# Products without a reader inside a blockwise inversion, and a reordered beginning of the first head group

## The chip, the cores and the metric

The kernel runs on one NeuronCore of a Trainium2 chip. The metric is device time in microseconds of one execution; the time before is 2007.33 us, the median of 3 runs from 2003.42 to 2015.3 us. TensorE (PE) multiplies, VectorE (DVE), ScalarE (ACT) and GpSimd (POOL) work elementwise, SyncE (SP) issues most transfers. Each engine runs its own instructions in order and waits on semaphores for the others.

## The reference, cut to what matters

512 tokens of width 1024 pass a first block (pooling, stick-breaking attention, a squared-ReLU MLP), then 16 meta tokens are put in front (T = 528) and a gated delta layer and a latent attention layer follow. The change touches the gated delta layer (16 value heads on 8 key heads, chunks of the sequence):

```python
def gdn_mixer(h, w_in, conv_w, a_log, dt_bias, out_norm, w_out):
    proj = h @ w_in
    qkv, z, b, a = ...                       # 4096, 2048, 16 and 16 columns
    qkv = jax.nn.silu(causal_depthwise_conv(qkv, conv_w))      # 4 taps
    q = l2norm(...) * (GDN_DK ** -0.5); k = l2norm(...); v = ...
    beta = jax.nn.sigmoid(b)
    g = -jnp.exp(a_log) * jax.nn.softplus(a + dt_bias)
    o = gated_delta_rule_chunked(q, k, v, beta, g)
    ...
def gated_delta_rule_chunked(q, k, v, beta, g):
    gc = jnp.cumsum(g, axis=-1)
    decay = jnp.exp(jnp.where(incl, gc[..., :, None] - gc[..., None, :], -jnp.inf))
    m = jnp.einsum('bhnid,bhnjd->bhnij', kb, k) * jnp.where(strict, decay, 0.0)
    sol = lax.linalg.triangular_solve(m + eye, rhs, left_side=True, lower=True, unit_diagonal=True)
    ...                                      # then a scan over the chunks
```

## The kernel before

Activations lie feature-major: 128 features on the partitions, 8 slices (kt) of a width of 1024, tokens along the columns. Products of weights and activations are kept near fp32 by splitting both into a high and a low part: `mm3` (L325 to L329) multiplies high by high, high by low and low by high. A weight panel of 128 output features is 512 KB; SP loads it (`refill`, L592), ACT writes its high half (`split_high`, L317), POOL its low half (`split_low`, L322), in a ring of four, and PE counts up `panel_used` when it is through. A projection of a panel over all 528 tokens is `project(j, b, k0, k1)`: 8 slices, each 2 halves of the tokens x 3 products = 6 products of 264 columns, 48 in all, into two PSUM banks.

The gated delta layer works in four groups of four value heads (`gdn_group`, g = 0 to 3, unrolled on every engine). The tokens form 5 chunks: 1 to 4 of 128 tokens, chunk 0 the 16 meta tokens. In each group:

- Panels 0 to 7 are projected (two of k, two of q, four of v). For each, DVE applies the four taps of the convolution (`taps`, L1477 and L1484), ACT and DVE the SiLU (`conv_exp`, `conv_clamp`, `lnexp`, `gated`), and for k and q a norm over the head (`l2_square`, `l2_sum`, `l2_rsqrt`, `l2_scale`).
- The decays: the running sums of the gates, one row per head and chunk, are split into high and low, written to a buffer in memory (`g_home`) and read back as rows (`decays_in`, L615). PE spreads them over a bank (`decay_rows`, L2169), ACT makes exp(-|difference|) of them (`decays`, L1002 and L1006).
- `first_m` (L1521) makes the matrices M of chunks 1 to 4 from the grams of k, the decays and beta. M goes through memory (`m_home`) to a layout with one 16x16 block per partition, in which POOL inverts the diagonal blocks by elimination (L693, L697); the inverses come back by way of `w_home`.
- The inversion: 15 steps, s = 0 to 14 (`STEPS`: levels 4, 5, 6, and in each the chunks 1, 2, 3, 4, 0), join blocks of 16 to 32, 64 and 128. A step is a product q (L2355, L2350 or L2359) with a mask times M from POOL (L721, L728), an ACT copy of it, one step later a second product (`join`: L2303, L2298, L2307), a DVE subtraction, and two steps later for levels 4 and 5 a transpose (`turn_u`, L2324) with a DVE copy (L1644). Level 4 is done in halves of 64, level 5 in quarters of 32 columns. PE runs them in program order; slices of a projection of z (`gate_slices`) stand between the steps from s = 9 on, the rest of it behind them.
- Then the scan over the chunks, with the projections of z, and the output projection of the group before.

The gates b and a are computed once, ahead of group 0: 8 slices of a product of 32 columns of weights into banks 6 and 7 as soon as each slice of the normalised input has its low half (`split_ready`), a copy (L935), transposes (L2119), a chain of small operations on ACT and DVE (`ba_act` counts ACT's to 11, `ba_dve` DVE's to 9), PE's running sums (L2126, L2129), their copies and the split of the sums (L955, L1457). Then ACT parks the residual in memory (`x_home`, L959), and group 0 begins. The group's own copies are of the rows of sm (L1466) and of the taps (L1469), counted in `g_smg`.

The lines that set the order around the change, on PE, at the beginning of a group and in the loop over the steps:

```python
                project(0, 0)
                pe.wait_ge(sem("rows_moved"), 16 + 64 * (g + 1))
                decay_rows(6, 1).then_inc(sem("g_gr"), 1)
                decay_rows(7, 2).then_inc(sem("g_gr"), 1)
                project(1, 2, 0, 4)
                ...
                for s, (l, c) in enumerate(STEPS):
                    ...
                    if s - 2 in TURNED:
                        turn_u(s - 2)
```

Of the kernel before, what the change touches and what calls it, by code (L numbers as in the profile page):

```python
# [5 lines left out]
F32 = mybir.dt.float32  # L6
FR = mybir.dt.float32r
BF16 = mybir.dt.bfloat16
ALU = mybir.AluOpType
# [83 lines left out]
GATE_FROM = 9  # L93
TURNED = [s for s, (l, c) in enumerate(STEPS) if not last_level(l, c)]
# [16 lines left out]
def build(nc, A, out):  # L111
    ctx = ExitStack()
    with ctx:
# [462 lines left out]
        def _(sp):  # L576
# [26 lines left out]
            def gdn_group(g, first):  # L603
# [165 lines left out]
        def _(act):  # L769
# [152 lines left out]
            with act.Fori(1, 3) as r:  # L922
# [11 lines left out]
            act.wait_ge(sem("ba_pe"), 1)  # L934
            act.activation(two(ba_f[0:32, :]), PS[0:32, 6:8, 0:HALF], ACT.Copy).then_inc(sem("ba_act"), 1)  # L935
            act.wait_ge(sem("ba_pe"), 2)
            act.activation(ba_e[:, 0, :, :], PS[:, 6, 0:160].rearrange("p (c n) -> p c n", c=CHUNKS)[:, :, 0:16],
                           ACT.Exp, scale=-1.0).then_inc(sem("ba_act"), 1)
            act.activation(al_e, rows_ab[:, 0:16], ACT.Exp).then_inc(sem("ba_act"), 1)
            act.wait_ge(sem("ba_dve"), 1)  # L940
            act.activation(ba_e[:, 2, :, :], ba_e[:, 1, :, :], ACT.Abs).then_inc(sem("ba_act"), 1)
            act.wait_ge(sem("ba_act"), 4)
            act.activation(ba_e[:, 2, :, :], ba_e[:, 2, :, :], ACT.Exp, scale=-1.0).then_inc(sem("ba_act"), 1)
            act.wait_ge(sem("ba_act"), 5)
            act.activation(ba_e[:, 2, :, :], ba_e[:, 2, :, :], ACT.Ln, bias=1.0).then_inc(sem("ba_act"), 1)
            act.wait_ge(sem("ba_pe"), 3)
            gcp = PS[:, 6, 0:160].rearrange("p (c a n) -> p c a n", c=CHUNKS, a=2)
            act.activation(sm[:, 2, :, :], gcp[:, :, 0, :], ACT.Copy).then_inc(sem("ba_act"), 1)
            act.activation(sm[:, 5, :, :], gcp[:, :, 1, :], ACT.Exp).then_inc(sem("ba_act"), 1)
            act.wait_ge(sem("ba_act"), 8)  # L950
            act.activation(sm[:, 3, :, :], sm[:, 2, :, :], ACT.Exp).then_inc(sem("ba_act"), 1)
            act.wait_ge(sem("ba_dve"), 7)
            act.activation(sm[:, 4, :, :], sm[:, 4, :, :], ACT.Exp).then_inc(sem("ba_act"), 1)
            act.wait_ge(sem("ba_pe"), 4)
            act.activation(decay_split[:, 0, :], PS[:, 7, 0:P], ACT.Copy).then_inc(sem("ba_act"), 1)  # L955

            for k in range(KT):
                act.wait_ge(*added("nB", k))
            act.dma_start(x_home, X).then_inc(sem("x_moved"), 16)  # L959

            def gdn_group(g, first):
# [32 lines left out]
                def decays(c):  # L994
# [4 lines left out]
                    act.wait_ge(sem("g_smg"), gst(g, 2, 1))  # L999
# [14 lines left out]
                decays(1)  # L1014
                decays(2)
                conv_exp(0)
                lnexp(0)
                split_ahead(1)
                l2_square(0)
                decays(3)  # L1020
                conv_exp(1)
                lnexp(1)
                split_ahead(2)
                l2_rsqrt(0)
                l2_square(1)
                conv_exp(2)
                l2_rsqrt(1)
                lnexp(2)
                decays(4)
                split_ahead(3)  # L1030
# [227 lines left out]
        def _(dve):  # L1258
# [163 lines left out]
            with dve.Fori(0, 3) as r:  # L1422
# [9 lines left out]
            ba = PS[:, 6, 0:160].rearrange("p (c n) -> p c n", c=CHUNKS)  # L1432
            dve.wait_ge(sem("ba_act"), 2)
            dt_row = rows_ab[:, 16:32].unsqueeze(1).to_broadcast([P, CHUNKS, 16])
            dve.tensor_tensor(ba_e[:, 1, :, :], ba[:, :, 16:32], dt_row, ALU.add).then_inc(sem("ba_dve"), 1)
            dve.tensor_scalar(ba_e[:, 0, :, :], ba_e[:, 0, :, :], 1.0, None, ALU.add).then_inc(sem("ba_dve"), 1)
            dve.wait_ge(sem("ba_dve"), 2)
            dve.reciprocal(sm[:, 0, :, :], ba_e[:, 0, :, :]).then_inc(sem("ba_dve"), 1)
            dve.wait_ge(sem("ba_act"), 6)
            dve.wait_ge(sem("ba_dve"), 1)  # L1440
            dve.scalar_tensor_tensor(out=ba_e[:, 1, :, :], in0=ba_e[:, 1, :, :], scalar=0.0,
                                     in1=ba_e[:, 2, :, :], op0=ALU.max, op1=ALU.add).then_inc(sem("ba_dve"), 1)
            dve.wait_ge(sem("ba_dve"), 4)
            dve.wait_ge(sem("ba_act"), 3)
            dve.tensor_tensor(ba_e[:, 1, :, :], ba_e[:, 1, :, :],
                              al_e.unsqueeze(1).to_broadcast([P, CHUNKS, 16]), ALU.mult).then_inc(sem("ba_dve"), 1)
            dve.wait_ge(sem("ba_dve"), 5)
            dve.tensor_scalar(sm[:, 1, :, :], ba_e[:, 1, :, :], -1.0, None, ALU.mult).then_inc(sem("ba_dve"), 1)
            gcp = PS[:, 6, 0:160].rearrange("p (c a n) -> p c a n", c=CHUNKS, a=2)
            dve.wait_ge(sem("ba_act"), 8)  # L1450
            dve.tensor_tensor(sm[:, 4, :, :], gcp[:, :, 1, :], sm[:, 2, :, :], ALU.subtract)\
               .then_inc(sem("ba_dve"), 1)
            dve.wait_ge(sem("ba_act"), 9)
            dve.tensor_tensor(sm[:, 3, :, :], sm[:, 3, :, :], sm[:, 0, :, :], ALU.mult).then_inc(sem("ba_dve"), 1)
            dve.wait_ge(sem("ba_dve"), 8)
            dve.wait_ge(sem("ba_act"), 11)
            dve.tensor_tensor(decay_split[:, 1, :], PS[:, 7, 0:P], decay_split[:, 0, :].bitcast(F32), ALU.subtract)\  # L1457
               .then_inc(sem("ba_dve"), 1)
# [3 lines left out]
            def gdn_group(g, first):  # L1462
                def tile_used(j):
                    p, i, length = gdn_panel(j, g)
                    dve.wait_ge(used, turn(p + 1, i, length))
                dve.tensor_copy(smg[:, :, :, :].rearrange("p a c n -> p (a c) n"),  # L1466
                                sm[:, :, :, bass.ds(4 * g, 4)].rearrange("p a c n -> p (a c) n"))\
                   .then_inc(sem("g_smg"), 1)
                dve.tensor_copy(cwg[:, :], conv_w[:, bass.ds(32 * g, 32)]).then_inc(sem("g_smg"), 1)  # L1469
                dve.wait_ge(sem("g_smg"), gst(g, 2, 2))  # L1470
# [85 lines left out]
                taps(0)  # L1556
                conv_clamp(0)
                gated(0)
# [372 lines left out]
        def _(pe):  # L1931
# [201 lines left out]
            def gdn_group(g, first):  # L2133
# [57 lines left out]
                if not first:  # L2191
                    pe.wait_ge(sem("g_vb"), gst(g, CHUNKS, 0))
# [597 lines left out]
```

## Time and profile before

| what | value |
|---|---|
| median of 3 runs | 2007.33 us |
| runs | 2003.42 to 2015.3 us |
| profiled execution, its own time | 2012.68 us |
| its span | 2010.9 us |
| mean granted clock of PE in it | 0.963 |
| PE busy | 1893.7 us (94%) |
| DVE, ACT, POOL busy | 961.1, 818.6, 688.2 us |
| first product of the gates, ahead of group 0 | 776.16 us of the span |

The profile is of one execution. Times are microseconds from the start of the span. PE is the matmul, PEld its weight load. The granted clock is 1.00 where PE may run at 2.4 GHz and 0.50 where it gets 1.2 GHz. Ends of matmuls are modelled, and consecutive ones overlap, so the distance from start to start is the time that one takes; a busy PE is not PE at its peak.

### The profile page before, as it was taken

To read this page: it belongs to the slowest core of one execution; us is meant where nothing else is said; L and a number is where in the kernel's file an instruction comes from. 1 tells how busy PE (TensorE), PEld (TensorE's weight loads), DVE (VectorE), ACT (ScalarE), POOL (GpSimd) and SP (SyncE) were. 2 spreads that over 40 slices of the span, in tenths; PEclk is the share of its full clock that TensorE was granted. 3 is DMA by queue.
4 is the path that set the end of the run, shared out by engine and by line. 5 is a ranking of instruction groups with operands and counts; after the bars stand their busy time and mean duration, and the time that the engine had idled before them with its cause. 6 is when DMAs were issued, how large, how long until landed. Compare 5 with 4: busy or idle time off the path is not lost.

```text
span 2010.9 us, 30195 instructions
## 1 busy us (share of the span) xinstructions
PE 1893.7 (94%) x11505; PEld 1570.7 (78%) x11641; DVE 961.1 (48%) x1657; ACT 818.6 (41%) x1478; POOL 688.2 (34%) x430
## 2 busy tenths in 40 slices
PE   6999999899999996998999999999988999999995
PEld 4677788678787875987989989998977777777774
DVE  6422213421111225656756763773665555555565
ACT  4555543342322223625624632551444334333432
POOL 3222244353434342450451270253134212322223
PEclk9999999999999998999999988996999999999998
DMA  5111223132323231220221330131132101111211
GB/s 179 53 53 53 63 94 105 42 115 75 114 82 106 74 104 57 77 75 1 88 75 32 87 85 12 53 98 43 43 107 70 56 32 53 63 54 51 73 42 53
DMA packets 72946, 140.43 MB, mean 70 GB/s; under 512 B 30561, under 2 KB 40289, under 8 KB 72577
## 3 DMA queue, kind: packets, MB, share of 16 engines
q1 hardware_dynamic: 72256, 133.98, 21.8%
q10 hardware_dynamic: 576, 4.87, 0.6%
q8 instruction: 80, 1.31, 0.3%
q14 instruction: 34, 0.27, 0.0%
HBM read 129.20 MB, written 9.63 MB: 69 GB/s over the span
## 4 chain that ended last, share of the span: by engine, by line
PE 45%; DVE 6%; POOL 4%; ACT 3%; issue 3%; DMA 1%; SPq 0%; POOLq 0%; ACTq 0%; DVEq 0%
PE ps L327 9%; PE ps L329 8%; PE ps L328 8%; PE ps L2646 4%; PE ps L2602 2%; POOL wsp L322 2%; PE ps L2609 2%; PE ps L2324 1%; PE ps L2636 1%; POOL ov L697 1%; POOL work L693 1%; DVE aux_f L1484 1%; PE ps L2307 1%; PE ps L2428 1%; PE ps L2359 1%
## 5 line engine op out<-in xcount | busy, mean ns | idle before, releaser
L322 POOL TENSOR_TENSOR wsp<-raw,wsp 128x1024 fp32r<-128x1024 f32 x231 | 556.4, 2413 | 1215.8 <-ACT wsp L317 1215.6
L327 PE MATMUL ps<-h_split,wsp 128*128 128x264 f32 (+1 forms) x1488 | 531.5, 357 | 18.8 <-DVE h_split L494 5.6
L329 PE MATMUL ps<-h_split,wsp 128*128 128x264 f32 (+1 forms) x1488 | 511.0, 343 | 0.0
L328 PE MATMUL ps<-h_split,wsp 128*128 128x264 f32 (+1 forms) x1488 | 510.8, 343 | 0.0
L327 PEld LDWEIGHTS ps<-h_split,wsp 128*128 128x128 f32 x1488 | 286.7, 193 | 65.7 <-issue 25.5
L328 PEld LDWEIGHTS ps<-h_split,wsp 128*128 128x128 f32 x1488 | 288.5, 194 | 32.7 <-issue 1.7
L329 PEld LDWEIGHTS ps<-h_split,wsp 128*128 128x128 f32 x1488 | 287.4, 193 | 32.3
L317 ACT ACTIVATE wsp<-raw 128x1024 fp32r<-128x1024 f32 x231 | 240.8, 1050 | 104.0 <-PE ps L329 102.8
L327 PE MATMUL ps<-y_split,wsp 128*128 128x512 f32 (+1 forms) x496 | 194.9, 393 | 11.9 <-DVE y_split L494 5.8
L328 PE MATMUL ps<-y_split,wsp 128*128 128x512 f32 (+1 forms) x496 | 191.5, 386 | 0.0
L329 PE MATMUL ps<-y_split,wsp 128*128 128x512 f32 (+1 forms) x496 | 191.3, 386 | 0.0
L327 PEld LDWEIGHTS ps<-y_split,wsp 128*128 128x128 f32 x496 | 94.5, 191 | 32.9 <-issue 11.6
L329 PEld LDWEIGHTS ps<-y_split,wsp 128*128 128x128 f32 x496 | 94.5, 190 | 19.2
L328 PEld LDWEIGHTS ps<-y_split,wsp 128*128 128x128 f32 x496 | 94.4, 190 | 18.7
L1418 DVE TENSOR_TENSOR work<-work,ps 128x512 f32<-128x512 f32 x32 | 22.0, 687 | 149.1 <-PE ps L329 149.1
L327 PE MATMUL ps<-y_late,wsp 128*128 128x264 f32 x256 | 77.7, 303 | 4.8 <-DVE work L1681 3.2
L2646 PE MATMUL ps<-ov 128*128 128x128 f32 (+1 forms) x448 | 80.5, 307 | 0.4 <-DVE ov L1909 0.3
L2646 PEld LDWEIGHTS ps<-ov 128*128 128x128 f32 (+1 forms) x448 | 60.6, 192 | 19.0 <-issue 10.9
L1484 DVE SCALAR_TENSOR_TENSOR aux_f<-ps,cwg,aux_f 128x528 f32<-128x528 f32 x96 | 73.8, 769 | 3.4
L328 PE MATMUL ps<-y_late,wsp 128*128 128x264 f32 x256 | 73.5, 287 | 0.0
L329 PE MATMUL ps<-y_late,wsp 128*128 128x264 f32 x256 | 73.3, 286 | 0.0
L914 ACT ACTIVATE work<-work 128x512 f32<-128x512 f32 x32 | 20.2, 633 | 122.5 <-DVE work L1410 122.5
(372 smaller groups left out, 2954.4 us busy)
## 6 DMA issues: line engine op xcount, KB each, us to landing
raw<-in_w SPq DMA_DIRECT2D x231, 512.0 KB, 3.5
m_home<-ov SPq DMA_DIRECT2D x16, 256.0 KB, 3.6
x_home<-x_res ACTq DMA_DIRECT2D x1, 2112.0 KB, 6.5
x_res<-in_x SPq DMA_DIRECT2D x4, 512.0 KB, 5.2
out<-x_res SPq DMA_DIRECT2D x8, 256.0 KB, 2.1
x_res<-x_home ACTq DMA_DIRECT2D x1, 1584.0 KB, 8.8
mats<-in_mats SPq DMA_DIRECT2D x1, 640.0 KB, 7.1
x_res<-x_home ACTq DMA_DIRECT2D x1, 528.0 KB, 4.1
```

Of the source, the lines that this page charges most:

```text
L317: act.activation(wsp[:, s, 0, :], raw[:, s, :], ACT.Copy).then_inc(hi_ready, 1)
L322: pool.tensor_tensor(wsp[:, s, 1, :], raw[:, s, :], wsp[:, s, 0, :].bitcast(F32), ALU.subtract).then_inc(lo_ready, 1)
L327: pe.matmul(o, wh, xh, start=start, stop=False)
L328: pe.matmul(o, wh, xl, start=False, stop=False)
L329: return pe.matmul(o, wl, xh, start=False, stop=stop)
L693: pool.tensor_tensor(tmp, w[:, k + 1:BLK, k:k + 1].to_broadcast([P, n, k]), w[:, k:k + 1, 0:k].to_broadcast([P, n, k]), ALU.mult)\
L914: act.activation(relu2[b], relu[b], ACT.Square).then_inc(sem("ff_sq"), 1)
L1418: dve.tensor_tensor(acc1[:, m, :], acc1[:, m, :], PS[:, m % 4, :], ALU.add)\
L1484: dve.scalar_tensor_tensor(out=shifted, in0=x, scalar=cwg[:, 4 * t + k:4 * t + k + 1], in1=shifted, op0=ALU.mult, op1=ALU.add)\
L2602: pe.matmul(PS[:, bank_, 0:hi_ - lo_], QN[:, h, P * i:P * i + P], KN[:, h, lo_:hi_], start=True, stop=False)
L2609: pe.matmul(PS[:, bank_, 0:hi_ - lo_], QR[r, h // 2, P * i:P * i + P], krope[r, lo_:hi_], start=False, stop=True)
L2646: last = pe.matmul(o_bank(b), VT[0:n, c, h * P:(h + 1) * P], PT[b][0:n, c, :], start=c == 0, stop=c == i + 1)
```

## The change

A table says how many products each step gets, and a helper issues them at the end of the step. They multiply the bf16 identity by itself and add into 128 columns of PSUM bank 7 that nothing reads:

```diff
+KEEP = [0] * 3 + [1] * 2 + [3] * 5 + [1] * 5
...
+                def keep_busy(count):
+
+                    for k in range(count):
+                        pe.matmul(PS[:, 7, HALF:HALF + P], mats_b[:, 0, :], mats_b[:, 0, :], start=False, stop=True,
+                                  skip_group_check=True)
...
                     if s - 2 in TURNED:
                         turn_u(s - 2)
+                    keep_busy(KEEP[s])
```

The second part concerns group 0. On PE the gates' product is interleaved with the first projection, slice by slice, and the later parts of the gates stand between parts of panel 1; the decay rows come behind panel 2, and the grams behind later waits. Groups 1 to 3 keep PE's order:

```diff
-            for kt in range(KT):
-                pe.wait_ge(*split_ready("n3", kt + 1))
-                w = [wba_all[:, part * 256 + 32 * kt:part * 256 + 32 * kt + P] for part in range(2)]
-                last = mm3t(pe, 6, *w, HS, kt, kt == 0, kt == KT - 1)
-            last.then_inc(sem("ba_pe"), 1)
...
+                if first:
+
+                    ready(0)
+                    for kt in range(KT):
+                        pe.wait_ge(*split_ready("n3", kt + 1))
+                        w = [wba_all[:, half * 256 + 32 * kt:half * 256 + 32 * kt + P] for half in range(2)]
+                        last = mm3t(pe, 6, *w, HS, kt, kt == 0, kt == KT - 1)
+                        if kt == KT - 1:
+                            last.then_inc(sem("ba_pe"), 1)
+                        last = mm3t(pe, 0, *part(0, kt), HS, kt, kt == 0, kt == KT - 1)
+                    last.then_inc(used, 1)
+                    project(1, 2, 0, 3)
+                    gates_turned()
+                    project(1, 2, 3, 6)
+                    decay_sums()
+                    project(1, 2, 6)
+                    pe.wait_ge(sem("g_conv"), 1)
+                    project(2, 0)
+                    pe.wait_ge(sem("rows_moved"), 16 + 64)
+                    pe.wait_ge(sem("ba_act"), 11)
+                    pe.wait_ge(sem("ba_dve"), 9)
+                    decay_rows(6, 1).then_inc(sem("g_gr"), 1)
+                    decay_rows(7, 2).then_inc(sem("g_gr"), 1)
+                    decay_rows(4, 3).then_inc(sem("g_gr"), 1)
+                    decay_rows(5, 4).then_inc(sem("g_gr"), 1)
+                    pe.wait_ge(sem("g_conv"), 2)
+                    project(3, 2, 0, 4)
+                    pe.wait_ge(sem("g_eabs"), 2 * HG)
+                    l2_sum(0)
+                    project(3, 2, 4)
+                    l2_sum(1)
+                    pe.wait_ge(sem("g_conv"), 3)
+                    project(4, 0, 0, 4)
+                    pe.wait_ge(sem("l2_done"), 2)
+                    pe.wait_ge(sem("g_eabs"), 3 * HG)
+                    for c in (1, 2):
+                        grams(4, c, 0).then_inc(sem("g_kk"), 1)
+                    project(4, 0, 4)
+                    pe.wait_ge(sem("g_eabs"), 4 * HG)
+                    for c in (3, 4):
+                        grams(4, c, 0).then_inc(sem("g_kk"), 1)
```

ACT and DVE hold the same operations of the gates as before, cut into functions and called in this order in group 0 (the split of the row sums now comes ahead of the other copies of the sums, and the parking of the residual, `park`, behind all of them):

```diff
+                if first:                      # ACT
+                    gates_front()
+                    split_ahead(1)
+                    gates_middle()
+                    conv_exp(0)
+                    decay_high()
+                    decay_sums()
+                    lnexp(0)
+                    decay_rest()
+                    park()
+                    l2_square(0)
+                    conv_exp(1)
+                    lnexp(1)
+                    split_ahead(2)
+                    l2_square(1)
+                    decays(1)
+                    decays(2)
+                    conv_exp(2)
+                    l2_rsqrt(0)
+                    lnexp(2)
+                    split_ahead(3)
+                    l2_rsqrt(1)
+                    decays(3)
+                    decays(4)
...
+                group_taps()                   # DVE
+                if first:
+                    dve.wait_ge(sem("g_smg"), 1)
+                    taps(0)
+                    gates_front()
+                    conv_clamp(0)
+                    decay_low()
+                    decay_rest()
+                    gated(0)
+                    dve.wait_ge(sem("ba_dve"), 9)
+                    dve.wait_ge(sem("ba_act"), 11)
+                    group_rows()
...
-                    sp.wait_ge(sem("ba_dve"), 9)      # SP, ahead of the write of g_home
+                    sp.wait_ge(sem("ba_dve"), 7)
```

In groups 1 to 3 the copy of the taps (L1469) now comes ahead of the copy of the rows (L1466), and the two waits on `g_smg` for the rows ask for 2 instead of 1.

## Rows read from the trace of the kernel before

**Rows 1.** The page: engines, the clock in 40 slices, the high-half group of ACT

```profile
PE 1893.7 (94%) x11505; PEld 1570.7 (78%) x11641; DVE 961.1 (48%) x1657; ACT 818.6 (41%) x1478; POOL 688.2 (34%) x430
...
PEclk9999999999999998999999988996999999999998
...
L317 ACT ACTIVATE wsp<-raw 128x1024 fp32r<-128x1024 f32 x231 | 240.8, 1050 | 104.0 <-PE ps L329 102.8
```

**Rows 2.** Stretches of 25 us: busy (instructions) by engine, PEclk, DMA share, GB/s

```profile
1025.00:1050.00 25.00, 24.43 (x350) 21.89 (x375) 10.35 (x31) 5.57 (x13) 13.81 (x9) 1.00 0.27 86
...
1200.00:1225.00 25.00, 24.96 (x150) 22.11 (x161) 4.11 (x11) 1.72 (x5) 1.85 (x1) 0.52 0.16 45
```

**Rows 3.** Two stretches in the inversion of group 2, columns as above

```profile
1184.00:1192.50 8.50, 8.11 (x180) 7.41 (x192) 6.60 (x18) 3.11 (x6) 6.08 (x8) 1.00 0.21 53
1192.50:1197.00 4.50, 4.38 (x80) 3.83 (x81) 2.15 (x7) 0.96 (x4) 4.50 (x3) 0.56 0.08 27
```

**Rows 4.** Timeline of DVE: start, us, line; the marks of the group lengths

```profile
952.79 2.42 DVE L1469 COPY cwg<-conv_w 128x32 f32<-128x32 f32 x1
...
1048.09 0.71 DVE L1554 COPY work<-ps 128x528 f32<-128x528 f32 x1 [1.85 <-PE ps L329]
...
1114.53 2.42 DVE L1469 COPY cwg<-conv_w 128x32 f32<-128x32 f32 x1
...
1288.32 2.41 DVE L1469 COPY cwg<-conv_w 128x32 f32<-128x32 f32 x1
...
1396.74 0.71 DVE L1554 COPY work<-ps 128x528 f32<-128x528 f32 x1 [3.42 <-PE ps L329]
```

**Rows 5.** Timeline of PE: where the inversions of groups 1 and 3 set in

```profile
1021.06 0.68 PE L2355 MATMUL ps<-aux_f,ov 64*64 64x64 f32 x16 [0.79 <-POOL aux_f L721]
...
1357.92 0.68 PE L2355 MATMUL ps<-aux_f,ov 64*64 64x64 f32 x16 [0.79 <-POOL aux_f L721]
```

**Rows 6.** Timeline of PE: bf16 products on the identity, and what follows

```profile
1567.48 0.28 PE L2614 MATMUL ps<-mats_b 128*128 128x128 bf16 x2
...
1567.58 0.47 PE L327 MATMUL ps<-h_split,wsp 128*128 128x512 f32 x1
```

**Rows 7.** Timeline of PE, beginning of group 0 ([...] idle before, releaser)

```profile
776.16 0.39 PE L327 MATMUL ps<-h_split,wba_s 128*128 128x264 f32 x1 [3.69 <-DVE h_split L460]
...
789.96 1.81 PE L2126 MATMUL ps<-sm,mats 16*128 16x16 f32 x8 [2.29 <-DVE sm L1448]
...
797.20 0.28 PE L328 MATMUL ps<-h_split,wsp 128*128 128x264 f32 x1
...
800.22 0.28 PE L329 MATMUL ps<-h_split,wsp 128*128 128x264 f32 x1
802.37 0.50 PE L2169 MATMUL ps<-decay_r,ones_r 2*128 2x512 f32 x2 [1.86 <-DMA decay_r<-g_home]
```

**Rows 8.** Timeline of DVE, same stretch

```profile
800.62 0.77 DVE L1477 TENSOR_SCALAR aux_f<-ps,cwg 128x528 f32<-128x528 f32 x1 [7.10 <-PE ps L329]
801.42 2.38 DVE L1484 SCALAR_TENSOR_TENSOR aux_f<-ps,cwg,aux_f 128x528 f32<-128x528 f32 x3
...
832.24 2.15 DVE L1521 SCALAR_TENSOR_TENSOR ov<-ps,sm,ov 128x128 f32<-128x128 f32 x8
```

**Rows 9.** Timeline of ACT: the parked tensor, a chunk's decays, a 528-column activation

```profile
792.77 0.35 ACTq L959 DMA_DIRECT2D x_home<-x_res  x1
...
802.96 1.14 ACT L1002 ACTIVATE ov<-ps,sm 128x128 f32<-128x128 f32 x4 [8.68 <-PE ps L2169]
...
807.49 0.65 ACT L551 ACTIVATE aux_f<-aux_f 128x528 f32<-128x528 f32 x1 [0.50 <-DVE aux_f L546]
```

**Rows 10.** Chain of waits: the two transfers of the row sums

```profile
793.33 6.68 DMA g_home<-aux
...
800.95 1.38 DMA decay_r<-g_home
```

**Rows 11.** A stretch of group 0, columns as in rows 2

```profile
816.90:871.30 54.40, 52.06 (x452) 50.78 (x456) 42.03 (x74) 29.61 (x50) 32.36 (x43) 1.00 0.34 91
```

More of the change, by code:

```diff
@@ L955, in _, with gates_front, gates_middle @@
[L955 to L959, printed above, removed]
+            def gates_front():
+                act.wait_ge(sem("ba_pe"), 1)
+                act.activation(two(ba_f[0:32, :]), PS[0:32, 6:8, 0:HALF], ACT.Copy).then_inc(sem("ba_act"), 1)
+            def gates_middle():
+                act.wait_ge(sem("ba_pe"), 2)
+                act.activation(ba_e[:, 0, :, :], PS[:, 6, 0:160].rearrange("p (c n) -> p c n", c=CHUNKS)[:, :, 0:16],
+                               ACT.Exp, scale=-1.0).then_inc(sem("ba_act"), 1)
+                act.activation(al_e, rows_ab[:, 0:16], ACT.Exp).then_inc(sem("ba_act"), 1)
+                act.wait_ge(sem("ba_dve"), 1)
+                act.activation(ba_e[:, 2, :, :], ba_e[:, 1, :, :], ACT.Abs).then_inc(sem("ba_act"), 1)
+                act.wait_ge(sem("ba_act"), 4)
+                act.activation(ba_e[:, 2, :, :], ba_e[:, 2, :, :], ACT.Exp, scale=-1.0).then_inc(sem("ba_act"), 1)
+                act.wait_ge(sem("ba_act"), 5)
+                act.activation(ba_e[:, 2, :, :], ba_e[:, 2, :, :], ACT.Ln, bias=1.0).then_inc(sem("ba_act"), 1)
@@ L961, in gdn_group, with decay_rest, park @@
+            def decay_rest():
+                act.wait_ge(sem("ba_dve"), 8)
+                act.activation(sm[:, 4, :, :], sm[:, 4, :, :], ACT.Exp).then_inc(sem("ba_act"), 1)
+            def park():
+                for k in range(KT):
+                    act.wait_ge(*added("nB", k))
+                act.dma_start(x_home, X).then_inc(sem("x_moved"), 16)
             def gdn_group(g, first):
@@ L998, in decays @@
                     e = AT[c][0:n, :, 0:n]
-                    act.wait_ge(sem("g_smg"), gst(g, 2, 1))
+                    act.wait_ge(sem("g_smg"), gst(g, 2, 2))
                     act.wait_ge(sem("g_gr"), gst(g, CHUNKS, k + 1))
@@ L1437, in _ @@
[L1437 to L1444, printed above, removed]
@@ L1465, in tile_used, with group_rows, group_taps @@
                     dve.wait_ge(used, turn(p + 1, i, length))
[L1466 to L1470, printed above, removed]
+                def group_rows():
+                    dve.tensor_copy(smg[:, :, :, :].rearrange("p a c n -> p (a c) n"),
+                                    sm[:, :, :, bass.ds(4 * g, 4)].rearrange("p a c n -> p (a c) n"))\
+                       .then_inc(sem("g_smg"), 1)
+                def group_taps():
+                    dve.tensor_copy(cwg[:, :], conv_w[:, bass.ds(32 * g, 32)]).then_inc(sem("g_smg"), 1)
                 def taps(t):
@@ L1554, in copy_z @@
                     dve.tensor_copy(two(zrow[t]), acc2((0, 2, 6, 6)[t])).then_inc(sem("z_copy"), 1)
-                taps(0)
-                conv_clamp(0)
-                gated(0)
+                group_taps()
[10 more added lines that the diff above has]
+                    group_rows()
+                else:
+                    group_rows()
+                    dve.wait_ge(sem("g_smg"), gst(g, 2, 2))
+                    taps(0)
+                    conv_clamp(0)
+                    gated(0)
                 taps(1)
@@ L2228, in gdn_group @@
+                    pe.wait_ge(sem("g_eabs"), gst(g, CHUNKS * HG, 3 * HG))
+                    for c in (1, 2):
+                        grams(4, c, 0).then_inc(sem("g_kk"), 1)
+                    project(4, 0, 0, 4)
+                    pe.wait_ge(sem("g_eabs"), gst(g, CHUNKS * HG, 4 * HG))
+                    for c in (3, 4):
+                        grams(4, c, 0).then_inc(sem("g_kk"), 1)
+                    project(4, 0, 4)
                 l2_sum(2)
@@ L2237, in gdn_group @@
                 pe.wait_ge(sem("g_m1"), gst(g, CHUNKS, 4))
[L2238 removed]
+                pe.wait_ge(sem("g_smg"), gst(g, 2, 2))
                 meta_decay_rows(5).then_inc(sem("g_gr"), 1)
```

196 lines of the change are left out of this document (93 added, 103 removed).

## The prediction

> **What bounds the kernel now.** I read the page first: the engine shares, then the line of granted clock over the 40 slices [rows 1]. TensorE is busy 1893.7 of 2010.9 us, no other engine much over half of that. So time is saved only where TensorE runs faster or waits less. The clock line shows the first kind: it stands at 9 nearly everywhere and sinks to 8 in slices 24 and 25 and to 6 in slice 28 (a slice is 50.3 us: 1156 to 1257 and 1357 to 1408 us), which is where the third and the fourth group of the gated delta layer (groups 2 and 3) run their inversions. It also stands at 8 in slice 16 (754 to 804 us), the beginning of group 0.
>
> The table of 25 us stretches says how deep: in the same part of the work group 1 has 1.00 (1025 to 1050 us) and group 2 has 0.52 (1200 to 1225 us), which is the lower of the two levels, 1.2 GHz, nearly all the time [rows 2]. The clock falls in the middle of the inversion, after 8.5 us in which TensorE was busy for 8.11 us: 180 instructions, mostly products of 32 or 64 columns, and transposes. In the 4.5 us behind it the clock averages 0.56 [rows 3]. TensorE had work all the time when the clock fell; what it had was small.
>
> What a fall costs is read off marks that every group has. From one copy of the taps (L1469) to the next, group 1 takes 1114.53 - 952.79 = 161.7 us and group 2 takes 1288.32 - 1114.53 = 173.8 us: 12.1 us more for the same work [rows 4]. Group 3 has no successor, so I take its piece from the third step of the inversion to the third copy of z: 1396.74 - 1357.92 = 38.8 us, against 1048.09 - 1021.06 = 27.0 us in group 1: 11.8 us [rows 4, 5]. Groups 0 and 1 run the inversion without such a long fall. Two falls, 23.9 us together.
>
> The second place is the beginning of group 0, read from the engines' timelines. TensorE waits 3.7 us for the first slice of the normalised input, 2.29 us inside the chain of the gates, and 1.86 us for the row sums to come back from memory; only at 802.37 do the decay rows start [rows 7]. VectorE meanwhile waits 7.10 us for the first projection [rows 8].
>
> **The 22 products.** Each of the four groups gets 1 product at steps 3 and 4, 3 at steps 5 to 9, 1 at steps 10 to 14: 2 + 15 + 5 = 22, each 128x128 bf16 on resident tiles, into a piece of bank 7 that nobody reads. They free no one and wait for no one, but they stand in TensorE's queue, and the inversion has no visible idle that would hide them. The nearest row is the mask product of the latent attention, same operands' shape: two of them start at 1567.48 and the next instruction at 1567.58, so 0.05 us each [rows 6]. That is the lower end. The upper end is what one lasts by itself, half of that row's 0.28 us, 0.14 us, if its weight load and its drain hide under nothing. I take 0.07 us, near the row where they follow other work: 22 x 0.07 x 4 = 6.2 us (ends 4.4 and 12.3). Below nothing it can't be, as nothing is taken out.
>
> What they may give back is the 23.9 us. They add whole-array work precisely where it was thin: the 17 products of steps 3 to 9 bring about 1 us of it into the two stretches of rows 3, 13 us in which those steps lie. Groups 0 and 1 show that the unchanged mix is able to hold 2.4 GHz, so the mix is near the edge and a little should tip it. No row shows how much is enough. I take it that both falls go.
>
> The Trainium skill, "TensorE: Matmul & The Clock Gate", section "HAM oscillation — how this bites in real kernels", puts lost clock down to gaps in which TensorE has nothing to run, and its remedy is to close gaps. Here there is no gap ahead of the fall [rows 3]. By that rule the products close nothing and bring nothing, and the sum would hold only their cost; that is the first rival below.
>
> **The reordered beginning of group 0.** Step by step from the same timelines.
> (a) The first projection now runs slice by slice beside the gates' product. Twelve products per slice at (800.22 - 797.20) / 25 = 0.12 us are 1.45 us, 11.6 us for 8 slices from 776.16, plus about 1.6 us for the first three at half clock: done at 789.4. Before, the first taps started at 800.62 [rows 7, 8]. They start 11.2 us earlier.
> (b) VectorE's part of the gates (reciprocal, softplus) now stands behind the first taps, 0.77 + 2.38 us: it can begin at 792.6 [rows 8]. It takes 2 us, then TensorE's sums, 1.81 us and half a us [rows 7]: 797.1. TensorE fills the time with panel 1 (48 x 0.12 = 5.8 us) and ends it at about 798.5. The stall of 2.29 us shrinks to about half a us.
> (c) The split of the row sums ends at 797.7, against 793.33 before: their write starts 4.4 us later. If both transfers take what they took (6.68 us, then down to 802.37) the rows are back at 806.8 [rows 7, 10]. If they took long because the parking of x_res had been issued 0.6 us ahead of them at 792.77 [rows 9, 10], which is now behind them, they come up to 2.4 us sooner, at 804.4, when panel 2 is done (798.5 + 5.8) and TensorE gets to them anyway.
> (d) With the rows at 804.4 to 806.8 and 1.0 us for the four of them, TensorE stands where it stood at 816.9: 9 to 11 us ahead.
> (e) What counts is when the matrices M are complete, since their trip through memory and GpSimd's elimination lead to the inversion. Before: 832.24 + 2.15 = 834.39 [rows 8]. After, from the rows on: decays of two chunks 2 x 1.75 = 3.5 us, seven 528-column activations at 0.65 = 4.5, a panel's high half 1.05, two vector operations and gated 2.1, taps 3.15 with 1.1 to the clamp's end, M 4.3 with gated 0.7: about 21 us [rows 1, 8, 9]. So M at 825.3 to 827.8, 6.6 to 9.1 us earlier.
> (f) From there on to the inversion TensorE is busy 52.06 of 54.40 us [rows 11], so a lead on GpSimd's chain alone would be worth only 2.3 us; but TensorE itself is 9 us ahead by (d), and both move. I take 8 us, as the two parts overlap in full. Ends: 3 us, if a wait in the new order eats TensorE's lead (the sums at `pe.wait_ge(ba_dve, 6)` hold up two thirds of panel 1, and the taps of panel 1 behind it), and 10.5 us. A stall that goes would be followed by the taps' chain on VectorE, which is late next. The other edits (group_taps ahead of group_rows, the counts of g_smg, SP's wait for 7 instead of 9) have no duration of their own: groups 1 to 3 keep their order.
>
> **Sum.** Against the profiled execution's own time, 2012.68 us (span 2010.9): 2012.68 - 12.1 - 11.8 + 6.2 - 8 = 1987.0. That execution is 5.3 us above the median of the runs, 2007.33, and the runs spread over 11.9 us, the size of one fall. If the falls go, most of that spread goes with them, so I leave the sum as it is and do not shift it by the 5.3 us.
>
> **Rivals.**
> 1. The products don't hold the clock. What is needed may be more than the 1 us that they bring, and then falls come as before. For it: nothing in the trace shows how much is enough. Against it: two of four groups hold without any. Time: median 2007.3 + 6.2 - 8 = 2005.5, or 2011 with exactly the profiled falls.
> 2. The clock is held but the reordering gains nothing, as the row sums come back late and the decays, at the head of ScalarE's queue, block the exponentials of the taps. Against it: 4.4 us later on a chain that has 11.2 us of head start. Time 1987 + 8 = 1995.
> 3. One of the two falls stays (the lowest point may lie in steps 0 to 4, which get 2 products): 1987 + 12 = 1999.
> 4. Slower: the products lengthen the thin stretch by 1 to 3 us in each group without counting as enough, and all four groups fall instead of two. Price 2 x 12 us: 2012.68 + 24 + 6.2 - 8 = 2035; with three falls 2023, still slower; from three on it decides. For it: groups 0 and 1 are near the edge too. Against it: whole-array work can hardly make a stretch thinner.
>
> **How the numbers follow.** Forecast 0.60, rival 1 0.20, rival 2 0.10, rival 3 0.05, rival 4 0.05. What a measurement of this kernel can tell from no change is about 0.5%, 10 us, given runs from 2003 to 2015: faster means under 1997. Faster is the forecast and rival 2, 0.70; rivals 1 and 3 lie inside, 0.25; rival 4 is slower, 0.05. The range: low 1979 (10.5 us from the order, products at 0.05 us, and shorter half-clock stretches in group 0), high 2006 (rival 1 at its median). The forecast's own range is 1981 to 1994.
>
> **What would show it.** Clock 1.00 in the 25 us stretches behind all four inversions, and the four pieces from step 2 to the third copy of z within 1 us of each other, at 28 to 29 us (27.0 plus the products). The product's line at 0.05 to 0.14 us from start to start. First taps near 789, decay rows near 805, M complete near 827, the third step's start in group 0 near 863. It is wrong if a stretch at 0.50 of more than 10 us stands in any group, if M is complete later than 832, or if the step with three products grows by more than 0.4 us.

## The result, and the profile after

| | before | changed |
|---|---|---|
| median of 20 executions each | 2019.55 us | 1993.6 us |
| lowest and highest | 1993.78, 2032.22 | 1977.44, 2009.06 |
| ratio, changed to before | | 0.9909, 95% interval [0.9881, 0.9936] |
| profiled execution, its own time | 2012.68 us | 1980.34 us |
| its span | 2010.9 us | 1978.6 us |

The change makes the kernel faster, by 0.9% as the ratio has it and by 1.3% (26.0 us) as the medians have it. The ratio, here and below, leaves out the executions that lie over 1.5% above the fastest of their kernel, 2 of the 20 changed and 7 of the 20 before, and with them some of the lost clock that the change is about. Both kernels spread over 30 us and more, and both profiles lie in the faster half of their kernel.

The page of the changed kernel, the lines that answer to [rows 1]:

```profile
PE 1864.7 (94%) x11593; PEld 1547.6 (78%) x11729; DVE 955.6 (48%) x1657; ACT 818.3 (41%) x1478; POOL 689.2 (35%) x430
...
PEclk9999999999999998999999999999999999999998
```

TensorE has 88 instructions more (4 x 22) and is busy 29 us less. The clock line has lost its 8 8 and its 6. The two stretches that answer to [rows 3], in the inversion of group 2 (stretch, its length, busy and instructions by engine, PEclk, DMA share, GB/s):

```profile
1173.60:1182.10 8.50, 8.12 (x171) 7.53 (x183) 6.34 (x18) 3.11 (x6) 6.08 (x8) 1.00 0.21 60
1182.10:1186.60 4.50, 4.39 (x108) 4.06 (x113) 2.69 (x9) 1.51 (x4) 4.50 (x3) 1.00 0.03 10
```

TensorE is as busy as before, and the clock stays at 1.00 where it had averaged 0.56. The marks of the groups, on VectorE's timeline, answer to [rows 4] (L1522 is the copy of the taps, L1606 the copy of z; lines have moved by up to 110):

```profile
944.15 0.17 DVE L1522 COPY cwg<-conv_w 128x32 f32<-128x32 f32 x1
...
1039.11 0.71 DVE L1606 COPY work<-ps 128x528 f32<-128x528 f32 x1 [1.85 <-PE ps L330]
...
1104.07 0.17 DVE L1522 COPY cwg<-conv_w 128x32 f32<-128x32 f32 x1
...
1266.96 0.18 DVE L1522 COPY cwg<-conv_w 128x32 f32<-128x32 f32 x1
...
1364.57 0.71 DVE L1606 COPY work<-ps 128x528 f32<-128x528 f32 x1 [1.85 <-PE ps L330]
```

and TensorE's third step of the inversion in groups 1 and 3, which answer to [rows 5]:

```profile
1010.86 0.68 PE L2465 MATMUL ps<-aux_f,ov 64*64 64x64 f32 x16 [0.79 <-POOL aux_f L722]
...
1336.34 0.68 PE L2465 MATMUL ps<-aux_f,ov 64*64 64x64 f32 x16 [0.79 <-POOL aux_f L722]
```

The piece from the third step to the third copy of z is 1039.11 - 1010.86 = 28.25 us in group 1 and 1364.57 - 1336.34 = 28.23 us in group 3; before it was 27.0 and 38.8 us. Groups 0 and 2 take 28.2 us as well. So the piece without a fall grew by 1.2 us, which is 22 products at 0.055 us, and the falls of 11.8 and 12.1 us are gone. Group 1 from copy to copy went from 161.7 to 159.9 us, group 2 from 173.8 to 162.9 us.

The difference of the two spans, 32.3 us, adds up so:

| where | us shorter |
|---|---|
| before group 0 | 1.6 |
| group 0: from the first operation of its norm's low half to the third step of the inversion, 97.4 to 90.7 us | 6.8 |
| groups 0 and 1: the same piece of inversion (group 0 had a dip of 3.4 us at half clock before) | 0.2 and -1.2 |
| group 1: from the copy of the taps to the third step, 68.3 to 66.7 us | 1.6 |
| the falls in groups 2 and 3, less the products | 10.8 and 10.6 |
| the rest | 1.9 |

Group 0 in detail. First VectorE, ScalarE and the chain of waits of the changed kernel, the lines that answer to [rows 8 to 10]:

```profile
788.23 0.77 DVE L1529 TENSOR_SCALAR aux_f<-ps,cwg 128x528 f32<-128x528 f32 x1 [4.25 <-PE ps L330]
...
824.21 2.16 DVE L1573 SCALAR_TENSOR_TENSOR ov<-ps,sm,ov 128x128 f32<-128x128 f32 x8
```

```profile
796.62 0.35 ACTq L975 DMA_DIRECT2D x_home<-x_res  x1
...
804.82 1.12 ACT L1018 ACTIVATE ov<-ps,sm 128x128 f32<-128x128 f32 x4
```

```profile
795.55 1.82 DMA g_home<-aux
...
799.86 4.18 DMA decay_r<-g_home
```

The taps start at 788.23 instead of 800.62, M is complete at 826.37 instead of 834.39. The write of the row sums took 1.82 us where it had taken 6.68, and the reading back ran until 804.04, with the parking of the residual (issued at 796.62) beside it.

### The profile page after: what moved, and what is told of

Read it like the earlier page. It is cut to its first block, busy times and chain, and to the rows that moved or that the text cites. A ratio compares the mean times of both kernels' runs of the same rounds, so it can differ in the third digit from the quotient of the medians.

```text
span 1978.6 us, 30374 instructions
## 1 busy us (share of the span) xinstructions
PE 1864.7 (94%) x11593; PEld 1547.6 (78%) x11729; DVE 955.6 (48%) x1657; ACT 818.3 (41%) x1478; POOL 689.2 (35%) x430
## 4 chain that ended last, share of the span: by engine, by line
PE 46%; DVE 5%; POOL 5%; issue 3%; ACT 2%; DMA 1%; SPq 0%; ACTq 0%; POOLq 0%; DVEq 0%
PE ps L328 10%; PE ps L330 9%; PE ps L329 9%; PE ps L2757 4%; PE ps L2713 2%; POOL wsp L323 2%; PE ps L2720 2%; PE ps L2747 1%; POOL ov L698 1%; PE ps L2434 1%; POOL work L694 1%; PE ps L2539 1%; PE ps L2570 1%; PE ps L2575 1%; DVE aux_f L1536 1%
## 5 line engine op out<-in xcount | busy, mean ns | idle before, releaser
L328 PE MATMUL ps<-h_split,wsp 128*128 128x264 f32 (+1 forms) x1488 | 523.7, 352 | 18.8 <-DVE h_split L495 5.6
L330 PE MATMUL ps<-h_split,wsp 128*128 128x264 f32 (+1 forms) x1488 | 505.0, 339 | 0.0
L329 PE MATMUL ps<-h_split,wsp 128*128 128x264 f32 (+1 forms) x1488 | 504.8, 339 | 0.0
L328 PEld LDWEIGHTS ps<-h_split,wsp 128*128 128x128 f32 x1488 | 281.8, 189 | 64.6 <-issue 25.5
L329 PEld LDWEIGHTS ps<-h_split,wsp 128*128 128x128 f32 x1488 | 282.5, 190 | 32.5 <-issue 1.6
L330 PEld LDWEIGHTS ps<-h_split,wsp 128*128 128x128 f32 x1488 | 281.6, 189 | 32.1
```

The lines of the kernel that those rows point to most:

```text
L328: pe.matmul(o, wh, xh, start=start, stop=False)
L329: pe.matmul(o, wh, xl, start=False, stop=False)
L330: return pe.matmul(o, wl, xh, start=False, stop=stop)
```

## The experiments

Each kernel is compared with the kernel before, run on the same chip beside it. "Falls" are stretches of more than 20 us at the granted clock of 0.50 that begin in an inversion, counted in the one trace per kernel, of its four groups; each lasted 31 or 34 us. The kernel before had medians of 2018.59 us beside experiments 1 to 4, 2013.36 us beside 5 to 8 and 2020.14 us beside 9 to 12, so a few us between medians of different rounds say little.

**1. The products alone.** The kernel before, with the table, the helper and its call, nothing else:

```diff
+KEEP = [0] * 3 + [1] * 2 + [3] * 5 + [1] * 5
...
                         turn_u(s - 2)
+                    keep_busy(KEEP[s])
```

> The kernel before with the 22 products per group alone; the beginning of group 0 and the order of the two copies as before. Theory A (the products make long falls of the clock rarer, at 0.055 us a product): from step 2 to the third copy of z 28.2 us in a group without a fall, instead of 27.0; cost 4.8 us over four groups; falls drop from about 2.5 per execution to about 1.2, so the time is about 11 us under the kernel before of the same rounds, and the mean granted clock of the fast executions near 0.975. Theory B (the falls became rarer only because the reordering shifted the groups in time): as many falls as before, about 5 us slower than the kernel before, mean clock near 0.962.

Median 2001.65 us against 2018.59, ratio 0.9936 [0.9900, 0.9972]. One of its 12 executions took 2148.07 us at a mean granted clock of 0.912; no trace of it was kept. One fall of four in the trace. Theory B is out: the products help in the old order too.

**2. The order alone.** The changed kernel with

```diff
-KEEP = [0] * 3 + [1] * 2 + [3] * 5 + [1] * 5
+KEEP = [0] * 15
```

> The changed kernel without any of the 22 products. Theory A: falls as often as before (2 or 3 long ones per execution, 12 us each), time about 2005 us where the kernel before has 2019, mean clock near 0.962; pieces without a fall 27.0 us. Theory B: falls stay rare, time about 1989 us, 5 us under the changed kernel, mean clock near 0.975. Under both the beginning of group 0 is 6 to 7 us shorter (M complete at 826 instead of 834 us).

Median 2000.92 us, ratio 0.9921 [0.9879, 0.9964]; one fall of four; the piece without one is 27.03 us. The time is between what the two theories gave but nearer to A's 2005 than to B's 1989. It can't be told from the changed kernel by the ratios (0.9921 and 0.9909, intervals that overlap); the granted clocks further down tell the two apart. Its median lies 17.7 us below the kernel before, and the order is worth 8.4 us where no clock falls (experiment 9). Whether the new order also makes falls rarer, or the rest is chance, stays open.

**3. More products.** `KEEP = [0] * 3 + [3] * 2 + [6] * 5 + [3] * 5`, 51 per group.

> The changed kernel with 51 products per group instead of 22 (3 at steps 3 and 4, 6 at steps 5 to 9, 3 at steps 10 to 14). Theory A, dose: cost 29 x 0.055 x 4 = 6.4 us, so an execution without a fall takes 1984 to 1986 us; falls become rarer still, median 1985 to 1990 us, spread under 10 us, clock 0.985. Theory C (the work that a product adds does not count, and the falls depend on something else, such as where the weights' copies or the transfers lie): falls as in the changed kernel, median 2000 us, clock 0.975.

Median 1992.09 us, from 1985.41 to 1994.51 in 6 executions, ratio 0.9864 [0.9812, 0.9917]. No fall of four; the pieces are 29.8 us in groups 1 to 3, 1.6 us over the changed kernel's, so 0.056 us for each of 29 more products. The dose works: the spread has shrunk from 32 to 9 us. The median lies 2 us above A's range of 1985 to 1990. The profiled execution took 1992.85 us without a fall, with more time at half clock outside the inversions than the changed kernel's trace has (82 against 65 us), so not all of the spread is the inversions'.

**4. The rows copied first again.** In groups 1 to 3 only:

```diff
-                group_taps()
                 if first:
+                    group_taps()
...
                 else:
                     group_rows()
+                    group_taps()
```

> The changed kernel with the copy of the rows ahead of the copy of the taps again in groups 1 to 3 (as before the change); group 0 as changed. Theory D (the second copy, of the taps, is held until the weights' split on GpSimd ends when it comes 0.14 us after that has begun, and the first taps of the group wait for it): the copy of the taps takes 2.4 us again in groups 1 to 3, and each group is 1 to 2.3 us longer, 3 to 7 us in all over the changed kernel, at the same number of falls. Theory E (DVE has slack there): the copy is long again but the groups keep their length, no difference.

Median 1997.12 us, ratio 0.9896 [0.9855, 0.9937], one fall of four: the medians can't tell it from the changed kernel. The trace can. Its VectorE at the beginning of group 1, and then its GpSimd:

```profile
944.58 0.21 DVE L1517 COPY sm<-sm 128x120 f32<-128x120 f32 x1
944.71 2.41 DVE L1522 COPY cwg<-conv_w 128x32 f32<-128x32 f32 x1
947.16 0.77 DVE L1529 TENSOR_SCALAR aux_f<-ps,cwg 128x528 f32<-128x528 f32 x1
```

```profile
944.58 2.51 POOL L323 TENSOR_TENSOR wsp<-raw,wsp 128x1024 fp32r<-128x1024 f32 x1 [63.53 <-ACT wsp L318]
```

The second copy lasts until GpSimd's instruction ends (944.71 + 2.41 = 947.12, 944.58 + 2.51 = 947.09), as before the change. From the first of the two copies to the third step group 1 takes 68.5 us, 66.7 in the changed kernel. In groups 2 and 3 that length is 69.3 to 69.7 us whether the copy was held up (group 3 here) or not (group 2 here), so VectorE has slack there. D and E each hold, D in group 1, E in groups 2 and 3: 1.8 us in all, under what D gave. Over all traces of this study the copy was held up in 10 of 12 groups that copied rows first and in none of 30 that copied taps first.

**5. The same 22 products at the late steps.** `KEEP = [0] * 10 + [5] * 2 + [4] * 3`.

> The changed kernel with its 22 products per group all at steps 10 to 14 (5, 5, 4, 4, 4), where slices of a projection already stand between the steps, and none at steps 3 to 9. Theory A (what counts is how thin the work is at steps 3 to 9, just ahead of the place where the clock falls): long falls as often as without products, so about 2005 us against the changed kernel's 1994, clock 0.965, pieces without a fall still 28.2 us. Theory B (any 22 products anywhere in the inversion do, for instance because they bring the dense rest sooner back to full clock): as the changed kernel, 1994 us, clock 0.975; a fall would then be shorter than 38 us.

Median 2007.84 us, ratio 1.0001 [0.9951, 1.0051]; three falls of four. Theory A: where they stand decides. At steps 10 to 14 they cost their time and prevent nothing, and they don't shorten a fall that has begun (31 to 34 us, against 31 before).

**6. The thin steps only.** `KEEP = [0] * 5 + [6] * 5 + [0] * 5`, 30 per group.

> The changed kernel with 6 products at each of steps 5 to 9 and none elsewhere, 30 per group. Theory A: cost 8 x 0.055 x 4 = 1.8 us over the changed kernel, an execution without a fall at 1979 to 1982 us; falls in the inversion as rare as with 51 products (none in four groups of that profile), median 1982 to 1990 us, clock 0.981. Theory F (steps 3 and 4 need cover as well, as the clock's record reaches back over them): falls as in the changed kernel, median 1994 to 1996 us.

Median 1982.87 us, from 1980.45 to 1989.28 in 6 executions, ratio 0.9818 [0.9778, 0.9858], against the changed kernel's 0.9909 [0.9881, 0.9936]. No fall of four. The two weren't run side by side, and against the medians of the kernels before beside them they stand closer, at 0.985 and 0.987. But all six executions lie under 1990 us, where 14 of the changed kernel's 20 lie above, and experiment 11, with the same table in another round, has 1982.51 us.

**7. Narrow products.** The changed kernel's table, with

```diff
-                        pe.matmul(PS[:, 7, HALF:HALF + P], mats_b[:, 0, :], mats_b[:, 0, :], start=False, stop=True,
+                        pe.matmul(PS[0:32, 7, HALF:HALF + 32], mats_b[0:32, 0, 0:32], mats_b[0:32, 0, 0:32], start=False, stop=True,
```

> The changed kernel with its 22 products cut to 32 rows, 32 columns of weights and 32 moving columns each: as many instructions in the same places, about a sixteenth of the array and a quarter of the columns. Theory A (array work counts): falls as without products, 2001 to 2005 us, clock 0.966; a product costs 0.03 to 0.05 us. Theory G (instructions on the engine's queue or the time between them count, not their size): as the changed kernel, 1992 us, clock 0.976.

Median 2037.54 us, ratio 1.0103 [1.0072, 1.0134], slower than the kernel before; four falls of four, and all 12 executions between 2031.69 and 2045.68. G is out. A named the direction, but too little: the narrow products don't merely fail, with them the clock falls in every group of the trace.

**8. The parking later.** The changed kernel with ScalarE's `park()` moved from behind `decay_rest()` to behind `lnexp(2)`.

> The changed kernel with the parking of the residual (2112 KB) put behind the exponentials of panel 2 on ScalarE, 15 us later, so that neither the write of the row sums nor their reading back meets it. Theory H (the parking sets how long the row sums take): the reading back falls from 4.18 to about 1.4 us, the decays start at about 802 instead of 804.8, M is complete 1.5 to 2.7 us earlier, and so is the inversion: 1.5 to 2.7 us under the changed kernel in group 0 of the trace. Theory I (the chain is held by TensorE's panel 2, which ends near 804): the rows are there earlier but M moves by less than 0.7 us. Falls as in the changed kernel, so the median can't tell it; the trace of group 0 does.

Median 1987.94 us of 6 executions, ratio 0.9821 [0.9767, 0.9875], one fall of four. In group 0, TensorE's waits between 785 and 830 us, of the changed kernel and then of this one:

```profile
PE ps L2235 <- DMA decay_r<-g_home: 1.8, 1, 1.8
```

```profile
PE ps L2221 <- ACT ov L1018: 1.8, 1, 1.8
```

The row sums come early enough now, TensorE's wait for them is gone, and it waits as long behind it, for ScalarE's decays, which start no sooner because a panel's high half and a square stand ahead of them in ScalarE's queue. From the copy of the taps to M complete it is 42.2 us against 42.6. Theory I as to the size (0.4 us), though the holder is ScalarE's queue and not TensorE's panel 2.

**9. The thin steps in the old order.** Experiment 1's kernel with experiment 6's table.

> The kernel before, in its old order, with 6 products at each of steps 5 to 9 (30 per group). Falls in the inversions are then gone on both sides, and the difference to the thin-steps kernel of the same order of steps is the reordering alone. Theory J (the order is worth what the traces add up to: 6.8 us in the beginning of group 0, 1.6 us from the copies in group 1, 1 to 2 us of chance): median 1992 to 1994 us against 1982.9, that is 9 to 11 us. Theory K (half of the reordering's gain in the medians was falls of the clock that the new order avoids): under 6 us apart, 1988 us.

Median 1991.28 us, from 1988.48 to 1994.63, ratio 0.9869 [0.9829, 0.9910]; no fall. Against experiment 6 that is 8.4 us: the value of the order with the falls out of the way, and close to the 6.8 + 1.6 us that the traces give it. Experiment 11, run in the same round as this one, gives 8.8 us, of which the later parking may be 0.4. That is just under J's 9 to 11 us and above K's 6: nearer to J.

**10. Long products on a corner of the array.** Experiment 6's table, 32 rows and 32 columns of weights, 128 moving columns:

```diff
+                        pe.matmul(PS[0:32, 7, HALF:HALF + P], mats_b[0:32, 0, 0:32], mats_b[0:32, 0, :], start=False, stop=True,
```

> The thin-steps kernel (6 products at steps 5 to 9) with each product cut to 32 rows and 32 columns of weights, but all 128 moving columns: as long on TensorE, a sixteenth of the array. Theory L (the share of the array counts): falls in most groups, 3 or 4 of 4 in the trace, 2025 to 2040 us as with the narrow products. Theory M (moving columns count, however small the array part): no falls, 1980 to 1985 us.

Median 2038.9 us, ratio 1.0108 [1.0068, 1.0147]; four falls of four. This and experiment 6 are the cleanest pair: same places, same number, same columns, only the part of the array differs. One piece each from the third step to the copy of z, group 0 of this kernel and group 1 of experiment 6's (stretch, its length, busy and instructions by engine, PEclk, DMA share, GB/s):

```profile
862.50:906.60 44.10, 43.48 (x440) 38.03 (x469) 12.15 (x37) 6.75 (x15) 15.06 (x11) 0.58 0.15 49
```

```profile
1012.80:1041.50 28.70, 28.30 (x440) 25.77 (x470) 12.24 (x36) 6.76 (x15) 15.32 (x12) 1.00 0.24 75
```

440 instructions of TensorE in both, busy for all but 0.6 and 0.4 us, and 15.4 us between them. Theory L. (Group 0 here and group 1 there: in experiment 6 the piece is 28.7 us in all four groups.) The thin steps' own small products and transposes were the same in all kernels; which of them count for little was not tried.

**11. The thin steps and the late parking.** Experiment 8's order with experiment 6's table.

> The thin-steps kernel with the parking of the residual behind the exponentials of panel 2: the two changes that looked best. 0.4 us from the parking as its trace showed: 1979 to 1983 us, not to be told from the thin-steps kernel's 1982.9; 1990 or more would say that the parking, now beside panel 3, brings a fall.

Median 1982.51 us, from 1980.22 to 1987.65, ratio 0.9823 [0.9782, 0.9863]; no fall. Not to be told from experiment 6, as expected.

**12. Whole weights, few columns.** Experiment 6's table, 128x128 weights, 32 moving columns.

> The thin-steps kernel with whole 128x128 weights but only 32 moving columns per product: whole array, a quarter of the columns, and a weight load each. Theory L (array share times columns counts): a quarter of the dose, less than the changed kernel's own 22 products give, so falls in 1 to 3 of 4 groups, 1995 to 2015 us. Theory N (the weight loads count): no falls, 1980 to 1985 us.

Median 1993.41 us, from 1982.6 to 2004.02, ratio 0.9885 [0.9838, 0.9931]; no fall in the trace, but three of the six executions are at 1997 us or more, as if with one, and a product costs 0.024 us. The median is where neither theory put it, between full cover (1983) and none. It is consistent with a dose that is smaller by the columns, so both the columns and the part of the array would count; a quarter as effective or a half can't be read from six executions.

Falls in the traces, put together:

| products per group | kernels | groups with a fall |
|---|---|---|
| none | before, 2 | 3 of 8 |
| 22 at steps 10 to 14 | 5 | 3 of 4 |
| 22 as changed | changed, 1, 4, 8 | 3 of 16 |
| 30 or 51, whole array, 6 at each of steps 5 to 9 | 3, 6, 9, 11 | 0 of 16 |
| 30 with whole weights and 32 columns | 12 | 0 of 4 |
| 22 or 30 on a 32x32 corner | 7, 10 | 8 of 8 |

Four groups per trace are few: 3 of 8 and 3 of 16 don't show by themselves that 22 products help. The mean granted clock was recorded for every execution, and its medians say it with more of them: 0.959 before and 0.966 with the order alone, 0.973 with the 22 products alone and 0.975 with both, 0.966 with the products late (0.963 before, in that round), 0.983 with 6 at each thin step.

## Why the prediction was right, and where not

The forecast was faster, 1987.0 us and a range from 1979 to 2006; the median is 1993.6. The mechanism was right, the certainty that it gave to the falls was not, and two errors cancelled. By its own steps:

- **The cause of the falls** (little work while TensorE is busy): right, and shown by experiments 6 and 10. TensorE had as many instructions in both and stood idle for 0.6 and 0.4 us; what kept the clock at 1.00 was the part of the array that the added products used.
- **"I take it that both falls go"**: half right, and the term that was mis-sized. In the profile none of four groups fell, but three more traces with the same 22 products had one fall each. The median of the changed kernel lies 13 us over its profile, about one fall. Its executions lie at 1977 to 1980 us (4 of them), at 1989 to 1996 (8) and at 1999 to 2009 (8). I read them as none, one and two falls; only the first has a trace of this kernel itself, and experiment 3 reached 1992.85 us without a fall, so the reading is an estimate. By it the forecast's case, no fall, came in about a fifth of the executions. Rival 3, one fall left at 1999 us, describes as many as the next eight, and had been given 0.05; rival 1, that the products bring too little, holds for the rest. By the prediction's own sign of being wrong, no stretch at 0.50 of more than 10 us in any group, the profile passes and the traces of experiments 1, 4 and 8 do not.
- **The reference was not the typical execution.** The sum was made against a profile of 2012.68 us with two falls; 20 executions have a median of 2019.55. The 5.3 us by which the profile lay above the first three runs pointed the wrong way. Both sides moved up by about as much, 6.9 and 6.6 us, so the difference came out as forecast, 26 us in the medians against 25.7. That agreement is luck: not two falls to none, but some falls fewer from a higher level. Less 8.4 us for the order and plus 4.9 for the products it leaves some 22 us for the clock, an estimate, close to the 23.9 of the sum.
- **The price of a product**: 0.055 us instead of 0.07, 4.9 instead of 6.2 us; the row with two mask products, 0.05, was the right one.
- **The order**: 8 us taken, 6.8 us measured in group 0, 8.4 us between experiments 9 and 6 with the copies. What stands ahead of group 0 ended 1.6 us sooner, which the sum did not have and no part of the change accounts for (the trace before has 10 us more at half clock in its first 80 us). With it (a) came at 788.2 for 789.4, (b) at 794.9 for 797.1, and for (d) TensorE is through the decay rows at 804.5, where it had stood at 816.7: 12.2 us for 9 to 11. Less the 1.6 all three are within 0.6 us. In (c) the write was short, as the second branch had it, but the reading back met the parking and took that time: the rows were there at 804.0 of 804.4 to 806.8. In (e) M was complete at 826.37 us, within the 825.3 to 827.8 forecast, but 1.6 of the 8.0 us are the earlier start, so the order gave 6.4 (and the terms listed there add up to 20.4 us, not 21). The third step of group 0 began at 863.00 us as forecast, again with the 1.6 us. What (e) did not say is that a sooner landing would gain nothing: experiment 8 removed that wait and ScalarE's queue took its place.
- **"groups 1 to 3 keep their order", no duration of their own**: wrong. The two copies had changed places, and I overlooked that the row shown for the first mark was itself a 2.42 us copy of 32 columns [rows 4] that takes 0.17 us elsewhere. It is worth 1.6 to 1.8 us, in group 1 alone (experiment 4). The Trainium skill, "SBUF — State Buffer", section "Who interferes with whom", says that a copy on VectorE in one of its two-port modes and a GpSimd instruction take the same pair of ports, and that whichever begins second waits for the end of the first. The traces agree as to the end, within 0.04 us (that the copy runs in such a mode no row shows); but in the changed kernel both copies begin up to 0.10 us behind GpSimd's instruction and run in 0.17 and 0.22 us, and twice one at 0.13 us or 0.14 us got through. So which copy was held can't be read from the order of the starts as the trace has them; it turned on the last tenth of a microsecond, and at 0.13 to 0.14 us it went either way.
- **Rival 4** (the products lengthen the thin stretch, four falls, 2035 us) did not happen to the products as they are, but its mechanism is real: on a corner of the array the same table makes four falls of four and 2037.54 us.
- **Rival 1** was drawn from the rule of the Trainium skill, "TensorE: Matmul & The Clock Gate", section "HAM oscillation — how this bites in real kernels", that gaps cost the clock. In experiment 10's piece TensorE is busy 43.48 of 44.10 us and the clock is at 0.58. The rule as told there doesn't cover this kernel; the measurement decides.

What stays open: how much whole-array work is enough. 3 products at each of steps 5 to 9 (with 1 at those around them) were not always, in 16 groups; 6 always were, in 16 groups. Nor was any size between the 32x32 corner and the whole array tried. And whether a group falls at the lower dose differs from execution to execution of the same program; nothing here shows what decides it.

## What to carry to other kernels

A stretch of small matmuls can lose TensorE's clock while TensorE is busy nearly all the time (8.11 of 8.50 us here), and the dense work behind it then pays: look for the granted clock by stage, not for idle time. If a few products are put in, they belong at the thinnest steps (here steps 5 to 9) and should use all rows and columns; on a 32x32 corner of the array they did harm, and sizes between were not tried. And where a kernel's spread is as large as the gain, a profile of one execution is one draw: count the events in several traces before a sum is anchored on one.

## What was not expected of the hardware

- The fall depends on the part of the array. Six products of 128 columns at each thin step, 128x128 weights: 0 falls in 12 groups (experiments 6, 9, 11). Same number and columns, 32x32 weights: 4 in 4 (experiment 10), more than with no products at all (3 in 8).
- A fall lasts once it has begun. The slices of a projection between the steps, dense work, did not end it: the clock came back after some 30 us, when the projection stood alone. In the groups without a fall the same mix of slices and steps ran at 1.00; why it holds the clock there and doesn't bring it back is open. In experiment 7, after the thin steps (stretch, length, then as above):

```profile
876.00:900.00 24.00, 23.74 (x157) 20.45 (x170) 3.63 (x11) 2.88 (x7) 4.66 (x3) 0.50 0.21 67
```

- A whole product among others costs 0.055 us, one of 32 columns with whole weights 0.024 us: the record of its weight load alone lasts 0.10 us, so the loads overlap with other work.
